# A hybrid attention layer in FP32 on Trainium2: the order of the copies, folds and projection fills in the second attention

## What is computed

```python
proj = x @ w_in                                   # q, k, v: 1024 columns each, f_logit: 16
q, k, v = (t.reshape(Bsz, S, 16, 64) ...)
log_f = jax.nn.log_sigmoid(f_logit + b_f)
c = jnp.cumsum(log_f, axis=1)
s = jnp.einsum('bhqd,bhkd->bhqk', qi, k) * scale
s = s + cqi[..., None] - c[:, :, None, :]
s = jnp.where(kpos[None, :] <= qpos[:, None], s, -jnp.inf)
o = jnp.einsum('bhqk,bhkd->bhqd', softmax(s), v)
```

## Time and profile before

| | |
|---|---|
| median of 3 runs | 2604.47 us (2603.03 to 2606.34) |
| the profiled execution's own time | 2602.32 us |
| its span in the trace | 2600.4 us |
| PE busy in the span | 2521.2 us, 97% |
| DVE, ACT, POOL busy | 1545.5, 1125.9, 1232.8 us |
| mean granted clock of PE | 0.994 of full |
| second attention | 1184 to 1731 us |
| of this, one pair with fills | 66.5 us |

### The profile page before, as it was taken

The page is one execution under the profiler, slowest core; times in us unless marked ns, Lnnn a source line. Parts: engine busy times, 40 slices in busy tenths (PEclk is TensorE's granted clock), DMA queues, the critical chain, the costliest instruction groups (busy, mean ns, idle before and its releaser), DMA issues. The chain is left out here.

```text
span 2600.4 us, 36769 instructions
## 1 busy us (share of the span) xinstructions
PE 2521.2 (97%) x11914; PEld 2051.9 (79%) x11914; DVE 1545.5 (59%) x2240; ACT 1125.9 (43%) x2050; POOL 1232.8 (47%) x964
## 2 busy tenths in 40 slices
PE   8999999999999999999999999989999999999989
PEld 5788888887788878888888888768778888878767
DVE  6455542355766775435555555555757777776774
ACT  4333233204666661126677767641433333344431
POOL 3788887444222124431111111135169888666672
PEclk9999999999999999999999999999999999999999
DMA  3222223587101004321111111322033333476551
GB/s 108 84 78 67 61 77 109 207 298 247 53 25 32 24 27 167 128 99 57 42 40 40 40 40 41 128 89 67 25 113 110 116 117 113 139 269 215 178 174 61
DMA packets 126490, 267.18 MB, mean 103 GB/s; under 512 B 13872, under 2 KB 14000, under 8 KB 126400
## 3 DMA queue, kind: packets, MB, share of 16 engines
q1 hardware_dynamic: 84800, 157.85, 19.0%
q10 hardware_dynamic: 41600, 108.19, 11.7%
HBM read 198.02 MB, written 67.96 MB: 102 GB/s over the span
## 5 line engine op out<-in xcount | busy, mean ns | idle before, releaser
L640 POOL TENSOR_SCALAR whi<-raw 128x512 fp32r<-128x512 f32 x194 | 149.9, 773 | 1079.3 <-PE bank L823 644.9
L642 POOL TENSOR_TENSOR wlo<-raw,whi 128x512 fp32r<-128x512 f32 x194 | 274.8, 1417 | 16.2
L760 PE MATMUL bank<-a_hi,whi 128*128 128x512 f32 x464 | 184.9, 398 | 3.8 <-POOL wlo L642 2.0
L760 PE MATMUL bank<-b_lo,whi 128*128 128x512 f32 x464 | 183.9, 396 | 0.0
L655 POOL TENSOR_TENSOR wlo<-a,whi 128x512 fp32r<-128x512 f32 x114 | 164.3, 1442 | 15.7 <-ACT whi L1639 15.0
L823 PE MATMUL bank<-b_hi,whi 128*128 128x512 f32 x384 | 154.9, 403 | 5.6 <-DVE fk_lo_odd L2405 3.2
L823 PE MATMUL bank<-b_hi,wlo 128*128 128x512 f32 x384 | 151.6, 395 | 0.0
L823 PE MATMUL bank<-b_lo,whi 128*128 128x512 f32 x384 | 151.3, 394 | 0.0
L760 PE MATMUL bank<-b_hi,whi 128*128 128x512 f32 x336 | 134.0, 399 | 3.5 <-ACT up_u L2022 3.1
L760 PE MATMUL bank<-a_hi,wlo 128*128 128x512 f32 x336 | 132.6, 395 | 0.0
L760 PE MATMUL bank<-a_lo,whi 128*128 128x512 f32 x336 | 132.6, 395 | 0.0
(11 more groups left out here) (707 smaller groups left out, 7771.9 us busy)
## 6 DMA issues: line engine op xcount, KB each, us to landing
raw<-in_w SPq DMA_DIRECT2D x206, 256.0 KB, 2.6
a<-in_pairs SPq DMA_DIRECT2D x152, 256.0 KB, 2.6
wd_scr<-wd SPq DMA_DIRECT2D x55, 256.0 KB, 4.6
wd<-in_down SPq DMA_DIRECT2D x44, 256.0 KB, 4.2
xs_scr<-made ACTq DMA_DIRECT2D x40, 256.0 KB, 2.6
fc<-c_scr ACTq DMA_DIRECT2D x16, 512.0 KB, 3.6
h_scr<-up_y ACTq DMA_DIRECT2D x13, 512.0 KB, 2.6
raw<-wd_scr SPq DMA_DIRECT2D x26, 256.0 KB, 2.7
```

Source lines behind the costliest of these rows:

```text
L640: nc.gpsimd.tensor_scalar(hi, src, 1.0, 1.0, ALU.mult, ALU.mult).then_inc(w_hi, 1)
L642: nc.gpsimd.tensor_tensor(lo, src, hi.bitcast(F32), ALU.subtract).then_inc(w_lo, 1)
L760: last = nc.tensor.matmul(psum_ap, ws[w][:, k, :], a[:, kt, hs(h)], start=(first and i == 0 and j == 0), stop=(final and i == n - 1 and j ...
```

## The change

Five things change, all in the second attention; no instruction is added or removed.

- **PE, start of a pair:** the transposes of V's first half move from behind parts 40 to 47 to behind part 44, and those of its second half move behind `scores(2)`.
- **PE, the step before a leaf** (steps 3, 7 and 9; at step 13 there are no scores left to issue): the parts that finish the leaf now come before `scores(s + 3)`.
- **ACT:** the first half of V is split before the second is copied out; `normalise(s + 1)` comes before the leaf's copies; `fold` moves behind `high` and `expo(s + 2)`; the K leaves' copies across (now `keys_across`) move to the same place.
- **DVE:** `maxima(s + 2)` comes before the leaf's low parts; `add` moves behind `low` and `inverse(s + 2)`.
- **Outside the pairs:** before the first pair the copies across follow each K leaf, as they did.

```diff
--- before.py
+++ after.py
@@ -1031,14 +1031,19 @@
                     pe.wait_ge(tile_out[h], it * 6 + (U_FOX + 3 * pp + 2))
                 pe.wait_ge(fx.q_lo, it * 8 + (4 * pp + 4))
                 pe.wait_ge(fx.k_twice, it * 8 + (4 * pp + 4))
+                def value_flip(h):
+                    pe.wait_ge(fx.lo, ch)
+                    flip_v(fx, flips[h], f_raw, h, it * 6 + (U_FOX + 3 * pp + 3))
+
                 scores(0)
                 scores(1)
-                for i in range(40, 48):
+                for i in range(40, 45):
                     forget_part(it, pp, i)
-                for h in range(2):
-                    pe.wait_ge(fx.lo, ch)
-                    flip_v(fx, flips[h], f_raw, h, it * 6 + (U_FOX + 3 * pp + 3))
+                value_flip(0)
+                for i in range(45, 48):
+                    forget_part(it, pp, i)
                 scores(2)
+                value_flip(1)
                 for s in range(NST):
                     flip_p(s)
                     if s and s % 2 == 0:
@@ -1046,13 +1051,15 @@
                     if not fills:
                         for i in PLE_EARLY.get(s, ()):
                             ple_part(i)
-                    if s + 3 < NST:
+                    if s + 3 < NST and not (fills and s + 1 in LEAVES):
                         scores(s + 3)
                     if not fills and s in PLE_LATE:
                         ple_part(PLE_LATE[s])
                     if fills:
                         for i in PARTS[s]:
                             forget_part(it if pp == 0 else it + 1, 1 - pp, i)
+                    if s + 3 < NST and fills and s + 1 in LEAVES:
+                        scores(s + 3)
                 values(NST - 1)
 
             pe.wait_ge(const_made, 3)
@@ -1467,13 +1474,16 @@
                     x = (f_q, f_k)[c][pp]
                     for hh, rows in enumerate(head_rows):
                         nc.scalar.activation(x[hh][rows, hs(h)], src[rows, :], ACT.Copy).then_inc(fx.q_hi, 1)
-                    if c == 1:
-                        for hh, rows in enumerate(head_rows):
-                            act.wait_ge(fx.q_hi, it * 16 + (8 * pp + 2 * i + hh + 1))
-                            nc.scalar.activation(x[hh][head_rows[1 - hh], hs(h)], x[hh][rows, hs(h)].bitcast(F32),
-                                                 ACT.Copy).then_inc(fx.k_twice, 1)
                 else:
                     nc.scalar.activation(f_raw[:, hs(h)], src[:], ACT.Copy).then_inc(tile_out[h], 1)
+
+            def keys_across(it, pp, i):
+
+                h, x = i % 2, f_k[pp]
+                for hh, rows in enumerate(head_rows):
+                    act.wait_ge(fx.q_hi, it * 16 + (8 * pp + 2 * i + hh + 1))
+                    nc.scalar.activation(x[hh][head_rows[1 - hh], hs(h)], x[hh][rows, hs(h)].bitcast(F32),
+                                         ACT.Copy).then_inc(fx.k_twice, 1)
 
             def sums_in(it, pp, hh):
 
@@ -1544,22 +1554,20 @@
                 expo(0)
                 normalise(0)
                 expo(1)
+                act.wait_ge(fx.pv, it * 16 + 8 * pp)
+                v_hi(fx, fv, flips[0][:], 0, it * 4 + 2 * pp)
                 forget_out(it, pp, 5)
-                act.wait_ge(fx.pv, it * 16 + 8 * pp)
-                for h in range(2):
-                    v_hi(fx, fv, flips[h][:], h, it * 4 + (2 * pp + h))
+                v_hi(fx, fv, flips[1][:], 1, it * 4 + (2 * pp + 1))
                 if not fills:
                     p_high(0)
                     p_load(1)
                 for s in range(NST):
+                    if s + 1 < NST:
+                        normalise(s + 1)
                     if fills and s in LEAVES:
                         forget_out(*following, LEAVES[s])
-                    if s + 1 < NST:
-                        normalise(s + 1)
                     if not fills and s - 1 in PLE_LATE:
                         ple_out(PLE_LATE[s - 1])
-                    if s and s % 4 == 0:
-                        fold(s - 1)
                     for n in CHUNKS_OF[s]:
                         high(n)
                     if not fills:
@@ -1567,6 +1575,10 @@
                             ple_out(i)
                     if s + 2 < NST:
                         expo(s + 2)
+                    if s and s % 4 == 0:
+                        fold(s - 1)
+                    if fills and s in LEAVES and LEAVES[s] in (2, 3):
+                        keys_across(*following, LEAVES[s])
                     if not fills:
                         if s == 0:
                             p_high(1)
@@ -1926,6 +1938,8 @@
                 sums_in(0, 0, hh)
             for i in range(2, 5):
                 forget_out(0, 0, i, bank[i % 2])
+                if i < 4:
+                    keys_across(0, 0, i)
             with act.Fori(0, NPAIR // 2 - 1) as it:
                 for pp in range(2):
                     forget_pair(it, pp, True)
@@ -2471,18 +2485,18 @@
                 for h in range(2):
                     v_lo(fx, fv, flips[h][:], h, it * 4 + (2 * pp + h))
                 for s in range(NST):
+                    if s + 2 < NST:
+                        maxima(s + 2)
                     if fills and s in LEAVES:
                         forget_out(*following, LEAVES[s])
-                    if s + 2 < NST:
-                        maxima(s + 2)
                     if not fills and s - 1 in PLE_LATE:
                         ple_out(PLE_LATE[s - 1])
-                    if s and s % 4 == 0:
-                        add(s - 1)
                     for n in CHUNKS_OF[s]:
                         low(n)
                     if s + 2 < NST:
                         inverse(s + 2)
+                    if s and s % 4 == 0:
+                        add(s - 1)
                     if not fills:
                         if s < PLE_KT:
                             p_low(s)
```

## The result

| | before, beside it | after |
|---|---|---|
| median of 6 runs | 2604.05 us (2600.43 to 2606.34) | 2615.48 us (2612.04 to 2617.15) |
| ratio after / before | | 1.0046, 95% interval 1.0036 to 1.0057 |
| profiled execution, its own time | 2602.3 us | 2617.15 us |
| its span | 2600.4 us | 2615.2 us |
| start of the second attention's first scores | 1184.08 us | 1186.15 us |

The change makes the kernel slower by 0.46%, 11.4 us. The spans differ by 14.8 us. The seven pairs account for 7 x 1.58 = 11.05, the last pair for 1.5, and what follows for 0.2.

A forecast was written before the change was run, and what follows sets the result against it. TensorE, busy 97% of the span, was taken as the bound, so only its waits counted. Seven pairs at 1.7 us (11.9) plus 1.0 for the last, on 2602.3, gave 2615.2; plus 2.1 for the median, 2617 us, range 2604 to 2627.

The forecast's parts named there:

- the side with 0.74: Whole kernel: slower by over 0.2%, chance 0.74.
- Start of the pair: Step 0's transposes, behind V's second-half transposes, start earlier: offset (after less before) -0.2 us.
- Leaf 0: Steps 3 to 5: PE's part newly waits until 1205.9; step 5's transposes start at 1207.4 without waiting, offset -0.6 us.
- Leaf 2: Steps 9 and 10: PE's part behind the leaf starts at 1228.8 against 1228.71, offset +0.1 us, wait about 1.1 us.
- The late fold: Steps 12 and 13: DVE's add ahead of maxima(15) leaves about 0.45 us; step 15's exponential comes at about 1239.35.
- Leaf 3: Step 14: scaling at 1240.8 ahead of the copies, PE's part at 1244.1 instead of 1242.40, offset +1.7 us a pair.
- Absolute: Step 14's wait swallows what comes before it in the pair; each of seven pairs is 1.7 us longer, 11.9 us.
- Last pair: Fold and add behind the exponential delay a maxima and a copy; with V's transposes, 1.0 us taken.
- The clock: Rival: the clock falls at step 14 in each pair for some 3 us, 12 us more, 2629 us; chance 0.12.
- Faster: Rival: waits at the transposes go and leaves cost nothing, 1.8 us a pair, 13 us, 2592 us; chance 0.12.
- Cancel: Rival: wins and losses cancel within 5 us, maxima(15) earlier by 0.5, step 10's wait half; 2604 to 2609; chance 0.14.

The follow-up runs named there:

- x3: Changed kernel with fold and add back ahead of the high and low parts at steps 4, 8 and 12; 2614.91 us, ratio 1.0046.
- x2: Changed kernel with leaf 3's copies on ACT back ahead of step 15's scaling; 2606.94 us, ratio 1.0015.
- x5: Kernel before with only step 15's scaling on ACT moved ahead of leaf 3's copies; 2615.97 us, ratio 1.0047.
- x4: Changed kernel with PE's scores back ahead of the parts that finish a leaf; 2611.86 us, ratio 1.0043.
- x7: Changed kernel with leaf 3's copies ahead of the scaling, folds and adds early, and scores ahead of the parts again; 2596.50 us, ratio 0.9961.
- x1: Changed kernel with a leaf's low parts on DVE back ahead of maxima(s + 2); 2621.14 us, ratio 1.0077.
- x9: x7 with the early folds and adds only in the pairs with fills, late in the last pair; 2595.20 us, ratio 0.9976.

## Why the prediction came out right

2617.0 us were predicted and 2615.5 measured, inside 2604 to 2627 and on the side with 0.74. By its steps:

- **Start of the pair** (offset -0.2): the part tried alone gave -0.36 a pair. Right in sign, a little small.
- **Leaf 0**: a new wait until 1205.9 was expected. The part starts at 1207.92 - 2.07 = 1205.85, and waits 0.44. Step 5's transposes were put at 1207.4 without a wait; they start at 1207.34 without one. Three durations and two latencies of other places in the trace, added to the start of a group of transposes, met it within 0.1 us.
- **Leaf 2**: expected at 1228.8; 1230.99 - 2.07 = 1228.92, after a wait of 1.36. In the later pairs the wait is 0.94 to 1.10 us, near the 1.1 that was named.
- **The late fold**: the step was too small, and its effect stood at a place that the prediction gave no wait. `maxima(15)` was to be later by about 0.45 and the exponential behind it by 0.25. The maxima start at 1240.27 - 2.07 = 1238.20 instead of 1237.45, later by 0.75, and the exponential at 1241.73 - 2.07 = 1239.66 instead of 1239.10, later by 0.56. Step 14's low part stands behind the maxima on DVE, so step 14's transposes wait 1.02 instead of 0.47, and start at 1240.31 instead of 1239.71. x3 shows the link: with the folds early the 0.47 is back.
- **Leaf 3**: the scaling was expected at 1240.8, the part behind it at 1244.1. Measured: 1243.20 - 2.07 = 1241.13, and 1246.42 - 2.07 = 1244.35. The copy follows the scaling's start by 1.06 and not by its whole 1.18, and the fold made the scaling late. The term that carries the sum was 1.7 us a pair; measured 1.58 in the mean (1.95 in the first pair, 1.56 to 1.70 in the next five, 1.00 in the seventh). The move of the scaling is 1.38 of it, by x2 and by x5.
- **"Absolute"**: this step failed. Leaf 3's wait was to swallow what comes before it. It moves with what comes before: 0.40 us of the folds (x3) and 0.66 of the scores (x4) reach the pair's end. The time was right nonetheless because the gains and losses up to leaf 2 nearly cancelled (+0.1 predicted, and 1228.92 - 1228.71 = +0.2 measured), and because the chain was worked out from the exponential on, which held a part of the fold's share. That this step did no harm is luck: with 0.66 us won ahead of leaf 3, as in x4, the same rule would have missed all of it. The sum by parts is -1.19 (what x7 keeps) + 1.38 + 0.40 + 0.66 = 1.25 against 1.58; the 0.33 left over is not placed by any run; it is what the parts cost together and not one by one.
- **Last pair**: 1.0 predicted, 1.5 seen, but nothing shows it to be the folds': the clock and the wait for the store make differences of this size between kernels with the same code there (x3 and x7).
- **The clock**: the wait was put at 1.4 us and is 1.65, and in the kernel after no pair shows a fall behind it, so the forecast was right to leave it out. The reason given, that so short a wait is harmless, is only half borne out: in x3 a wait of 1.67 us was followed by the lower clock in two pairs of seven, at 1.5 us each, while in x5 the same 1.67 was followed by it in none. The rule cited beside it (the Trainium skill, TensorE: Matmul & The Clock Gate, The HAM clock gate), by which the low clock is the default and only activity lifts it, goes with x3's two pairs; it doesn't say which of such waits will do it, and no run here does.
- **Faster** fell: it needed ACT 1.5 us ahead at leaf 3, and ACT's exponential came 0.56 later than before. What the change does at the start of the pair and with the maxima ahead of the leaves' low parts was a gain all the same, 1.19 us a pair, and x7 shows it: with three places left as they were, the kernel is 0.4% faster than before.
- **Cancel** fell: the wait at leaf 2 was not the half but the whole of mine, and `maxima(15)` went back, not forward.

## What to carry to other kernels

On an engine that works in order, a copy that frees a buffer for TensorE's next matmul goes ahead of a scaling whose user comes a step later, above all when the scaling must wait for a reciprocal: the copies use that wait, and what they delay the scaling beyond it (0.9 us here) costs nothing while its user isn't yet due. A change of several moves is to be taken apart before it is dropped: here one move of one instruction costs 1.38 us a pair, more than the 1.19 that the useful ones bring. And where an experiment shows no gain in the mean, look at the periods one by one; two disturbed ones of seven hid what the other five had won.

## What the runs showed of the hardware

- Waits of 1.6 to 1.7 us between dense matmuls can go either way: in the kernel after, x1, x4 and x5 none of the seven was followed by a pair drawn out by the clock, in x3 two of seven were. Where it came, the mean clock was 0.56 over 3.4 us, near the 1.2 GHz level, and cost 1.5 us. In x7 and x9, with no wait over 0.62 us in a pair, it came in none. In the last pair the kernel before's 1.80 us at a side product was followed by it, while the kernel after's 2.35 us at the same product wasn't (the part starts at 1691.61, and from 1691.6 to 1695.0 the granted clock is 1.00). So the length of a wait alone doesn't decide it.
- The last pair's length goes by its mean granted clock (0.94, 0.92 and 0.90 above) and by when the store of the side product lands (7.5 us behind its issue in x3, 8.9 in x7), over 4.7 us in kernels of nearly the same code. A few microseconds between profiles of this kernel are no evidence unless they stand in most of the seven pairs.
- An ACT copy behind a scaling of 1024 columns starts 1.05 to 1.06 us behind its start, though the scaling is shown with 1.15: neighbours on one engine overlap by about a tenth of a microsecond. A sum over starts, not over durations, gives the right total.
